# A paged attention score on VectorE alone: sixteen multiply-and-sum instructions a page in place of GpSimd's product and one reduction

## What is computed

```python
k_past = cache_k[page_table].reshape(db, n_pages * PAGE_SIZE, SB_HEADS, SB_HD)
...
z = jnp.einsum('bqhd,bkhd->bhqk', qblk, k).astype(jnp.float32) * scale + bias_f
```

## Time and profile before

| | |
|---|---|
| Median of 3 runs | 1200.21 us (1195.49 to 1201.98) |
| Profiled execution | 1200.28 us, of which the span is 1198.6 us |
| PE busy | 952.1 us (79%) |
| DVE busy | 745.0 us (62%), 781 instructions |
| POOL busy | 379.1 us (32%), 189 instructions, 312.4 us of them the page products |
| ACT busy | 359.2 us (30%) |
| HBM | 216.18 MB read, 190 GB/s over the span |

### The profile page before, as it was taken

One profiled execution on the slowest core, in us unless ns is written; L12 is line 12 of the kernel. 1 busy time (PEld: TensorE's weight loads), 2 busy tenths in 40 slices (PEclk: granted clock), 3 DMA queues, 4 the chain that ended last, 5 costly groups with the idle time before them and its releaser, 6 DMA issues.

```text
span 1198.6 us, 15002 instructions
## 1 busy us (share of the span) xinstructions
PE 952.1 (79%) x5561; PEld 713.2 (60%) x5561; DVE 745.0 (62%) x781; ACT 359.2 (30%) x575; POOL 379.1 (32%) x189
## 2 busy tenths in 40 slices
PE   4799867989877868678787789777868878689895
PEld 3566545767755656556687789543434333279894
DVE  4453226658659998999999998644323233055554
ACT  4212246322231333321223222353322323033433
POOL 5000003321025977767873589300000000002120
PEclk9689878999877998899998999778878878879997
DMA  9938842421134655567665887605777796623212
GB/s 357 317 104 297 310 165 88 141 93 58 62 129 168 213 176 158 176 204 252 229 213 200 274 287 257 213 0 185 272 286 291 277 333 250 232 71 106 71 36 72
DMA packets 111161, 228.27 MB, mean 190 GB/s; under 512 B 7249, under 2 KB 70328, under 8 KB 111088
## 3 DMA queue, kind: packets, MB, share of 16 engines
q1 hardware_dynamic: 53184, 167.41, 39.2%
q10 hardware_dynamic: 57904, 59.90, 15.5%
HBM read 216.18 MB, written 11.11 MB: 190 GB/s over the span
## 4 chain that ended last, share of the span: by engine, by line
PE 37%; DVE 21%; issue 12%; DMA 7%; POOL 5%; ACT 5%; SPq 3%; ACTq 0%; POOLq 0%; DVEq 0%
PE pp L1417 11%; PE pp L1420 7%; DVE zall L1094 6%; POOL slot L522 4%; DVE w_lo L940 4%; DMA vslot<-in_cache_v_dram 4%; PE pp L1781 4%; DVE slot L1093 3%; PE pp L1766 3%; PE pp L1742 3%; DMA w_raw<-in_gla_w_in_dram 3%; SPq L421 2%; SPq L435 2%; PE pp L1790 1%; PE pp L1635 1%
## 5 line engine op out<-in xcount | busy, mean ns | idle before, releaser
L522 POOL TENSOR_TENSOR slot<-slot,qb 128x1024 f32<-128x1024 f32 x112 | 312.4, 2809 | 251.5 <-DMA slot<-in_cache_k_dram 210.4
L940 DVE TENSOR_TENSOR w_lo<-w_raw,w_hi 128x1024 fp32r<-128x1024 f32 x94 | 169.3, 1803 | 55.7 <-ACT w_hi L583 55.7
L1094 DVE TENSOR_REDUCE zall<-slot 128x16 f32<-128x1024 f32 x128 | 151.3, 1208 | 0.5
L1420 PE MATMUL pp<-xa_hi,w_hi 128*128 128x512 f32 x264 | 116.3, 440 | 38.4 <-DVE w_lo L940 38.4
L583 ACT CAST w_hi<-w_raw 128x1024 fp32r<-128x1024 f32 x94 | 97.8, 1042 | 122.9 <-PE pp L1420 63.9
L1417 PE MATMUL pp<-xb_hi,w_hi 128*128 128x260 f32 x512 | 106.6, 290 | 32.9 <-DVE w_lo L940 22.8
L1420 PE MATMUL pp<-xa_lo,w_hi 128*128 128x512 f32 x264 | 111.7, 423 | 0.0
L1420 PE MATMUL pp<-xa_hi,w_lo 128*128 128x512 f32 x264 | 111.3, 422 | 0.0
L510 POOL COPY sqacc<-work 128x520 f32<-128x520 f32 (+1 forms) x5 | 3.4, 690 | 317.4 <-ACT work L598 317.4
L1417 PE MATMUL pp<-xb_lo,w_hi 128*128 128x260 f32 x512 | 103.8, 284 | 0.0
L1417 PE MATMUL pp<-xb_hi,w_lo 128*128 128x260 f32 x512 | 103.8, 284 | 0.0
(11 more groups left out here) (282 smaller groups left out, 1635.2 us busy)
## 6 DMA issues: line engine op xcount, KB each, us to landing
slot<-in_cache_k_dram SPq DMA_DIRECT2D x128, 512.0 KB, 4.7
slot<-in_cache_v_dram SPq DMA_DIRECT2D x64, 512.0 KB, 4.8
vslot<-in_cache_v_dram SPq DMA_DIRECT2D x64, 512.0 KB, 5.9
w_raw<-in_gla_w_in_dram ACTq DMA_DIRECT2D x12, 1024.0 KB, 5.5
slot<-in_gla_w_in_dram SPq DMA_DIRECT2D x24, 512.0 KB, 7.9
w_raw<-in_w_ple_gate_dram ACTq DMA_DIRECT2D x8, 1024.0 KB, 5.1
w_raw<-in_sb_w_in_dram ACTq DMA_DIRECT2D x8, 1024.0 KB, 5.5
w_raw<-in_w_kv_dram ACTq DMA_DIRECT2D x8, 1024.0 KB, 6.3
```

Source lines behind the costliest of these rows:

```text
L522: nc.gpsimd.tensor_tensor(slot[s][:], slot[s][:], qb[:, (n // NPG) % 2, :], ALU.mult).then_inc(S("k_mul_pool"), 1)
L940: nc.vector.tensor_tensor(lo, raw, hi.bitcast(F32), ALU.subtract).then_inc(S("w_split"), 1)
L1094: nc.vector.tensor_reduce(zall[:, n % NPG, b * SH:(b + 1) * SH], at.rearrange("p (h d) -> p h d", d=HD), AX.X, ALU.add).then_inc(S("k_used ...
L1420: last = nc.tensor.matmul(bank[m % 2], w[:, k, :], x[:, 0:NP_TOK], start=(k == 0 and first), stop=(k == KT - 1 and w is wl))
```

## The change

POOL's function and the rule that picks its pages are gone. DVE does all 128 pages, and in another form: for each head one instruction that multiplies 64 columns of the page by the query and sums the products into one column of `zall`.

```diff
-            def multiply_pages(job):
-
-                for n in pages_at(job):
-                    if on_pool(n):
-                        s = SLOT_OF[NSB + n]
-                        pool.wait_ge(S("qb_in"), n // NPG + 1)
-                        pool.wait_ge(S(f"slot_in{s}"), 16 * SLOT_TURN[NSB + n])
-                        nc.gpsimd.tensor_tensor(slot[s][:], slot[s][:], qb[:, (n // NPG) % 2, :],
-                                                ALU.mult).then_inc(S("k_mul_pool"), 1)
...
                     at, b = slot[SLOT_OF[NSB + n]][:], n // NPG
-                    if on_pool(n):
-                        dve.wait_ge(S("k_mul_pool"), pool_pages(n + 1))
-                    else:
-                        dve.wait_ge(S("qb_in"), b + 1)
-                        dve.wait_ge(S(f"slot_in{SLOT_OF[NSB + n]}"), 16 * SLOT_TURN[NSB + n])
-                        own.then(nc.vector.tensor_tensor(at, at, qb[:, b % 2, :], ALU.mult))
-                    nc.vector.tensor_reduce(zall[:, n % NPG, b * SH:(b + 1) * SH], at.rearrange("p (h d) -> p h d", d=HD),
-                                            AX.X, ALU.add).then_inc(S("k_used"), 1)
+                    dve.wait_ge(S("qb_in"), b + 1)
+                    dve.wait_ge(S(f"slot_in{SLOT_OF[NSB + n]}"), 16 * SLOT_TURN[NSB + n])
+                    for h in range(SH):
+                        c = slice(h * HD, (h + 1) * HD)
+                        last = nc.vector.tensor_tensor_reduce(at[:, c], at[:, c], qb[:, b % 2, c], 1.0, 0.0, ALU.mult, ALU.add,
+                                                              accum_out=zall[:, n % NPG, b * SH + h:b * SH + h + 1])
+                    last.then_inc(S("k_used"), 1)
```

More of the change, by code:

```diff
@@ L120, in pages_at @@
     return range(PAGES_THROUGH.get(job - 1, 0), PAGES_THROUGH[job])
[L123 to L130, removed]
 def query_job(b):
@@ L528, in _ @@
             nc.gpsimd.memset(attT[:], 0.0).then_inc(S("att_zero"), 1)
-            for j in range(PHASES["v"][0], PHASES["wo0"][0]):
-                multiply_pages(j)
-            for i, name in enumerate(("wo0", "ple0")):
+            for i in range(2):
                 for u in range(8):
-                    multiply_pages(PHASES[name][0] + u)
                     sum_squares((1 + i) * KT + u)
-            for j in range(PHASES["q1"][0], PHASES["up1"][0]):
-                multiply_pages(j)
             pool.wait_ge(S("k_used"), NPAGES)
```

## The result

| | before | after |
|---|---|---|
| Median | 1201.1 us (4 runs, 1195.49 to 1202.15) | 1219.58 us (4 runs, 1216.21 to 1222.9) |
| Span of the profiled execution | 1198.6 us | 1221.2 us |
| DVE busy, its instructions | 745.0 us, 781 | 784.1 us, 4733 |
| POOL busy | 379.1 us | 66.7 us |

What follows compares the result with a forecast made beforehand. DVE's work was taken to bound 371 to 763 us: 377 us come and 248 go, so 129 us more, plus 10 before it, make 139 us on 1200.3 us: 1339 us, range 1265 to 1500 us.

Steps and rivals of the forecast that it cites:

- What bounds the kernel: From 371 to 763 us, where 115 of 128 pages are scored, DVE's work (371.7 of 392 us) is the time.
- What goes, 248 us: 371 to 763 us: DVE loses 80 us of stretching, 39 of its page products and 129 of reductions.
- third rival: In the stretch something other than POOL slows the splits, so 80 us don't come back: 1419 us, chance 0.03.
- What comes, 115 x 3.28 us: DVE, 371 to 763 us: 115 pages of sixteen pairs (product and read-out) at 205 ns a pair, 377 us.
- Edits at nothing: Counted as costing nothing: POOL's work leaving, its earlier sums of squares, page loads, slots freed 2.2 us later.
- The lower bound: A pair on DVE at best: 134 ns product plus 16 ns read-out, 150 ns, 2.4 us a page.
- Before 371 us, 10 us: Before the stretch 13 pages gain 2.2 us each, 28 us on DVE, of which 10 us were taken to show.
- PE's waits should roughly double: Sign: PE's waits for the low part of the weights, 61.1 and 27.5 us before, should roughly double.
- sixth rival: PE at its lower clock becomes the bound, up to 1.5 us a job in 32 jobs: 1387 us at most.
- first rival: Summing product on DVE runs at half rate, 272 ns a pair, 4.35 us a page: 1467 us, chance 0.15.
- not-slower rival: In the stretch DVE's relief outweighs the pairs, below 135 ns each; at 120 ns 1173 us, chance 0.03.
- fourth and fifth rival: Fourth: a cheap pair of 150 ns on DVE, 1236 us, chance 0.05. Fifth: the not-slower rival, chance 0.03.

Runs made afterwards that it cites:

- experiments 2 and 3: experiment 2, and two runs of the changed kernel: sixteen instructions a page over 32 columns each (1164.33 us), or eight over 128 (1157.51 us).
- experiment 2: Changed kernel with sixteen 64-column products a page that keep no sum, so no read-outs, and one fill a page: 1197.19 us.
- experiment 10: POOL's additions of squares replaced by copies that read one operand: 1201.19 us in the changed kernel, 1196.45 us in the kernel before.
- experiment 6: Kernel before, with POOL filling its 112 slots with zeros instead of multiplying them: 1129.86 us, ratio 0.9403.

## Why the prediction was wrong

- **What bounds the kernel**: right. The growth of 20 us lies in the forecast stretch, DVE is busy there at 98%, and in experiments 2 and 3 the time followed 115 pages times what the timeline gave for a page.
- **What goes, 248 us**: right. The splits came back to 1224 ns (1220 forecast), xb_lo to 758 (760), xa_lo to 743 (760), g1T to 705 (700). The account of DVE's busy time closes with it within 2 us. The third rival is out.
- **What comes, 115 x 3.28 us**: this is the step that failed, and the sum owes 109 of its 119 us too many to it: 115 x 16 x 59 ns. I took a pair as a main instruction that hands over after 135 to 175 ns and a read-out that then holds the engine for 30 to 70. The first was at its lower bound (134 forecast at best, 137 measured without a sum). The second holds the engine for about 10 ns, by experiment 2: the read-out starts with the next product and runs beside it. The row that I followed, ScalarE's read of its own sum, stood alone, with nothing behind it to overlap. The rows of DVE that I had, a fixed part of 67 ns between neighbours (the subtraction, 610 - 545, gives 65) and fills of one column every 16 ns, were the nearer ones; their ends gave 150 ns, 4 ns above what was measured. The one-sided reading was to place 205 between 150 and 405 by another engine's row, where the same engine's rows lay at the low end.
- **Edits at nothing** said that POOL's additions come earlier and nobody hurries them. They block pairs, 16 us of DVE's time (the timeline of wo0, and experiment 10). In the kernel before those of wo0 began beside a reduction, which they can't hold up, and ended in the product after it. Timeline of the kernel before:

```profile
383.48 2.33 DVE L1094 TENSOR_REDUCE zall<-slot 128x16 f32<-128x1024 f32 x2
384.92 1.28 POOL L513 TENSOR_TENSOR sqacc<-sqacc,work 128x512 f32<-128x512 f32 x1 [3.04 <-ACT work L598]
385.74 1.02 DVE L949 SCALAR_TENSOR_TENSOR xa_lo<-hT,gcol,xa_hi 128x512 fp32r<-128x512 f32 x1
```

The product takes 1.02 us there, 0.3 over its 743 ns; in ple0 the additions ended in a split, 0.56 us. Together they cost DVE some 7 us before, and 16 now. The 14 us of idle time that DVE lost as it became busier hid the error in the sum.

- **The lower bound** was itself 4 ns too high, since it charged the read-out with the 16 ns of a fill, where about 10 were measured. That matters little: with 150 ns the sum gives 1234 us (the prediction's 1236 has 278 us for 115 x 2.4 = 276), still 15 above the measurement, of which 115 x 16 x 4.5 ns = 8 us are the pair and 5 the next point.
- **Before 371 us, 10 us**: about 1 showed. The 13 pages there cost DVE little more (127.8 us busy in place of 127.4), since the relief of its other instructions pays for them too.
- **PE's waits should roughly double**: they did not, 93 us in place of 89, as the stretch grew by 20 us and not by 129. PE's granted clock in the stretch went from 0.94 to 0.92 and its busy time from 317.5 to 326.7 us for the same work. That is the sixth rival in a small size; with DVE busy at 98% it can have set little of the time.
- **The rule on half rate** (first rival, 0.15) is out for this instruction: 1.03 ns a column from 32 to 128 columns. The other figure of the Trainium skill (Perfetto Trace Analysis, Optimizing Scalar/DVE Operations), some 60 ns for each DVE instruction, gave an estimate of 187 ns when charged to both halves of a pair; charged to the product alone it would give an estimate of 127, and 146 lies between. The product without a sum took 137.
- **The not-slower rival** decided at 135 ns a pair and had 0.03. With 146 the change was 11 ns a pair, or 20 us, from it. So the direction came true by a small margin, and nearer to the other side than 0.03 says: the chances of the fourth and fifth rival together should have been those of a bound from the same engine, not of a mishap.

## What to carry to other kernels

The cost of a short instruction is its start-to-start time in a run of its like, not its duration: here 146 ns for two instructions of 226 and 89 ns. A form that reads its operand once but splits it into sixteen pays sixteen fixed parts of 80 ns, and at 64 columns that eats nearly all of the second pass it saves (2.33 against 2.38 us a page). Before moving work off GpSimd because it stops VectorE, look for the place where it doesn't: inside three reductions of DVE its 2.4 us cost nothing, and inside two about 0.2 us. With 63 pages on GpSimd, 47 of them placed so, the kernel took 1164 us where the change took 1220.

## What the hardware showed that was not expected

- The read of DVE's summing register (`DVE_READ_ACCUMULATOR2_ANT`, 72 to 108 ns) runs beside the next product, which itself sums; by the comparison with a product that keeps no sum (137 against 146 ns) it costs about 10 ns of the engine.
- One POOL product (two operands in SBUF, 2.4 us) and one DVE instruction with two operands in SBUF exclude each other. It blocks, and doesn't slow: a 64-column product went from 0.22 to 2.41 us, the next was at 0.22 again. Reductions of 1024 columns beside such a product, and DVE instructions that take one operand from PSUM (L963 before, at most 0.70 us, 26 of them beside such a product) were not held up. On POOL's side one operand is enough: its copies of 0.62 us hold up a pair as well (0.66 us), its fills, which read nothing, don't (experiment 6).
- Small instructions are hit more often than large ones, as each POOL product finds another: 256 pairs lost 51 us, where the sixteen large products they replaced had lost 16 x (2438 - 1216) ns = 20 us. Of the 31 us more, the splits got 12 back.
